# Eight stage buffers instead of four for the projected pieces, and a denser start of their schedule in block 0

## The reference, cut to what matters

```python
h = x + concat(retention(...), window_attention(...)) @ w_out     # columns from rms_norm(x) @ w_in, w_in: 1024 x 2816
xt = rms_norm(h)
q  = (xt @ peer_w_q)                       # 8 heads x 2 halves of 128
s  = einsum(q, peer_sub_keys)              # 128 scores per head and half; top 16, then the best 16 of 256 pairs
idx, gates = ...                           # 128 experts of 16,384 for each token
hh = einsum('thkd,td->thk', peer_u[idx], xt)
a  = gelu(hh) * gates
y  = final_rms_norm(h + einsum('thk,thkd->td', a, peer_v[idx]))
```

## Time and profile before

| | us |
|---|---|
| median of 3 runs | 3061.26 |
| the 3 runs | 3061.08, 3061.26, 3069.75 |
| the profiled execution | 3069.51 |
| its span, first to last instruction | 3067.7 |

### The profile page before, as it was taken

How to read it: one execution, slowest core, us unless ns; L and a number is a source line. 1 busy time by engine, 2 the same in 40 slices (tenths; PEclk the granted TensorE clock), 3 DMA queues, 4 the chain that set the end, 5 groups by cost and what they waited for, 6 DMA issues and landing times.

```text
span 3067.7 us, 29063 instructions
## 1 busy us (share of the span) xinstructions
PE 2262.4 (74%) x8810; PEld 972.3 (32%) x8810; DVE 2035.3 (66%) x4942; ACT 1024.9 (33%) x3215; POOL 1188.2 (39%) x1052
## 2 busy tenths in 40 slices
PE   8888969877798777866687567756785568678564
PEld 6566713554235532332222122212221122211111
DVE  2483446865578655788558965697568765886865
ACT  2222522334233243323433343233432342332322
POOL 0022234424443333433344444444444444444442
PEclk9999988988799888966788788978887789879867
DMA  8589999999999999989999999999999999999997
GB/s 325 195 323 380 347 418 408 422 384 379 420 418 421 371 390 421 415 367 387 423 421 421 407 421 421 418 403 422 421 418 404 416 421 419 402 409 422 418 408 322
DMA packets 194446, 1213.93 MB, mean 396 GB/s; under 512 B 25384, under 2 KB 44368, under 8 KB 60144
## 3 DMA queue, kind: packets, MB, share of 16 engines
q0 software_dynamic: 148608, 1082.20, 86.0%
q1 hardware_dynamic: 45680, 129.87, 11.0%
HBM read 1192.28 MB, written 20.23 MB: 395 GB/s over the span
## 4 chain that ended last, share of the span: by engine, by line
DMA 38%; PE 34%; DVE 14%; issue 6%; ACT 4%; POOL 3%; SPq 1%; POOLq 0%; DVEq 0%; ACTq 0%
DMA ring<-in_peer_uv,idxg 31%; PE ps L916 15%; PE ps L878 7%; DVE ring L1651 7%; PE ps L659 6%; DMA proj_scratch<-wo 5%; POOL ring L584 3%; PE ps L859 2%; ACT ring L980 2%; DVE columns L1505 1%; DVE columns L1556 1%; DMA wo<-in_w_in 1%; PE ps L676 1%; DVE columns L1498 1%; PE ps L632 1%
## 5 line engine op out<-in xcount | busy, mean ns | idle before, releaser
L584 POOL DMA_INDIRECT ring<-in_peer_uv,idxg x1024 | 1172.8, 1145 | 1663.8 <-PE ps L916 1421.2
L916 PE MATMUL ps<-ring 128*64 128x512 f32 x4096 | 1242.2, 738 | 661.9 <-ACT ring L980 660.8
L1651 DVE SCALAR_TENSOR_TENSOR ring<-ring,xlo 128x1024 f32<-128x1024 f32 x512 | 626.6, 1224 | 412.9 <-DMA ring<-in_peer_uv,idxg 402.9
L1651 DVE SCALAR_TENSOR_TENSOR ring<-ring,xhi 128x1024 f32<-128x1024 f32 x512 | 626.3, 1223 | 389.7 <-DMA ring<-in_peer_uv,idxg 380.5
L916 PEld LDWEIGHTS ps<-ring 128*64 128x64 f32 x4096 | 291.1, 158 | 1458.8 <-ACT ring L980 987.2
L1161 ACT ACTIVATE small<-small 128x2 f32<-128x2 f32 x512 | 103.9, 203 | 1577.2 <-DVE ring L1651 1572.9
L659 PE MATMUL ps<-wo 128*128 128x176 f32 x1728 | 304.2, 334 | 72.5 <-ACT wo L980 45.7
L659 PEld LDWEIGHTS ps<-wo 128*128 128x128 f32 x1728 | 280.1, 203 | 135.6 <-issue 71.7
L980 ACT ACTIVATE ring<-gdiag,small 128x64 f32<-128x64 f32 x1024 | 300.3, 340 | 16.8
L980 ACT ACTIVATE gdiag<-fold,gateg 128x64 f32<-128x64 f32 x1024 | 292.8, 333 | 1.5
L878 PE MATMUL ps<-keyw,work 128*128 128x512 f32 (+1 forms) x576 | 268.8, 611 | 1.1 <-ACT work L980 1.1
(11 more groups left out here) (199 smaller groups left out, 1541.2 us busy)
## 6 DMA issues: line engine op xcount, KB each, us to landing
wo<-in_w_in SPq DMA_DIRECT2D x44, 704.0 KB
ring<-in_peer_uv,idxg POOLq DMA_INDIRECT x1024
wo<-in_w_out SPq DMA_DIRECT2D x4, 4096.0 KB
columns<-proj_scratch SPq DMA_DIRECT2D x7, 1536.0 KB, 12.8
ring<-in_w_in SPq DMA_DIRECT2D x7, 1408.0 KB, 8.0
proj_scratch<-wo SPq DMA_DIRECT2D x112, 88.0 KB
ring<-in_wqT SPq DMA_DIRECT2D x16, 512.0 KB, 4.1
h<-in_x_prompt SPq DMA_DIRECT2D x9, 512.0 KB, 8.3
```

The source lines that it names most:

```text
L584: nc.gpsimd.indirect_dma_start(row[r], None, A["peer_uv"], bass.IndirectOffsetOnAxis(ap=experts, axis=0)).then_inc(ld_row[r], 16)
L916: mm = nc.tensor.matmul(acc[side * HP:(side + 1) * HP, n * 512:(n + 1) * 512], row_u[r][:, 0:HP], row_v[r][:, n * 512:(n + 1) * 512], star ...
L1651: ins = stt(row_u[r], row_u[r], 1.0, (xlo, xhi)[unit % 2][:], ALU.mult, ALU.mult, accum_out=dot[:, r:r + 1])
```

## The change

Eight stage buffers take the place of four (five in `wo`, three in a new tensor `stg_more`), and so eight store semaphores the place of four. The ticks of pieces 8 to 47 are new: 16 pieces (q 8 to 23) stand at ticks 1 to 13, where 12 stood, and 24 pieces (q 24 to 47) at ticks 14 to 43, where 28 stood up to tick 44. The ticks of loads and stores follow from these. Pieces 48 to 127 keep their ticks, with eight buffers.

```diff
-STG = 4
+STG = 8
@@ def late_tick(q):
     if q < EARLY:
-        return 1 + (q - AHEAD) * 9 // 8
+        return 1 + (q - AHEAD) * 13 // 16 if q < 24 else 14 + (q - 24) * 31 // 24
@@
+        stg_more = sb("stg_more", [P, 3 * LW])
@@
         xT_early = part(3 * D)
-        stg_early = [part(LW) for _ in range(STG)]
+        stg_wide = [stg_more[:, i * LW:(i + 1) * LW] for i in range(3)]
+        stg_early = [part(LW) for _ in range(STG - 3)] + stg_wide
@@
         xT_late = part(4 * D + KC * SPAD)
-        stg_late = [part(LW) for _ in range(STG)]
+        stg_late = [part(LW) for _ in range(STG - 3)] + stg_wide
```

## The result

The changed kernel takes 3045.84 us (median of 6 runs, 3042.02 to 3050.84), the kernel before 3062.51 us (6 runs beside them). The ratio is 0.9940, 95% interval 0.9924 to 0.9957: 18 us faster, between 13 and 23 (the medians lie 16.7 us apart). Forecast were -23 us and 3038 us; the time lies in the range. Timed once more later, the ratio was 0.9941 (0.9925 to 0.9957).

What follows compares the result with a forecast made beforehand. Nearly the whole kernel was taken as bound by the bytes its gathers bring through saturated DMA engines (421 GB/s). Block 0's -11 and the late pieces' -6 and -6 make -23 us, from 3061.3 to 3038 us, range 3024 to 3060.

Steps and rivals of the forecast that it cites:

- the ceiling of 43 us for 153 us of waits: Whole kernel: ACT's store waits total 152.8 us, but lost DMA rate behind them caps the gain at some 43 us.
- The late pieces, -12 us: Two groups of late pieces at the ends of blocks: store waits go, -6 us each, bounds 0 and 14.4 and 14.6.
- the two dips that it took: Late pieces: rate dips of 9.3 and 9.0 us following the longest store waits; two thirds counted as gain, -6 us each.
- The two at the turns: Late pieces: dips of 5.1 and 5.6 us put down to the block's turn itself and left out of the gain.
- Block 0, -11 us: Block 0's early pieces: the last piece comes at 369 instead of 380 us, -11 us, bounds -20.8 and +2.
- The store waits that go in this part are hidden by the saturated engines, so I count no gain: Block 0's dense front, pieces 8 to 23: removing store waits there was priced at no gain.
- PE's own time for the four, 10 us, lies in PE's idle time there: Block 0's front: four added pieces, 4 x 2.6 = 10 us on PE, fit its idle time (busy 48.9 of 70 us).
- +5 was forecast for the front: Block 0's front: added weight loads and stores and later weights bring pair 7 at 259 instead of 254.02 us.
- Behind pair 7: 126 to 110 us forecast: Block 0, pair 7 to last early piece: PE's work gives 107 us, transfers 110.5; 110 taken instead of 126.
- The saving of 8.4 us: Block 0 behind pair 7: PE's idle times of 4.31 and 4.09 us, both behind ACT's store waits, were to go.
- the slow rival: Block 1's columns land late behind piece 23 and hold DVE's dots; at 297 us, +11, 3072 us; chance 0.06.
- The cover of 3 to 6 us: Block 0: columns landing at about 270 us leave some 3 to 6 us before pair 10 at about 276; priced at 0.

Runs made afterwards that it cites:

- ticks only: The kernel before with the new ticks and still four stage buffers: 3068.92 us, ratio 1.0019 to the kernel before.
- late on four: The changed kernel, but pieces 48 to 127 use four stage buffers again, pieces 0 to 47 keep eight: 3057.27 us, ratio 0.9983 to the kernel before.
- thin weights: Nine weight loads of block 0's front cut from 704 to 88 KB: 3036.47 us against the changed kernel, 3034.28 us with eight buffers and old ticks.
- its twin: The kernel before with eight stage buffers for the late pieces (48 to 127) only, old ticks and four buffers for pieces 0 to 47: 3050.68 us, ratio 0.9952.
- the buffers alone: The changed kernel with the old ticks, so eight stage buffers only: 3045.54 us, ratio 0.9953 to the kernel before.
- columns early: Eight buffers and old ticks, with block 1's columns set to load in block 0 at tick 12 instead of 14: 3044.92 us, ratio 0.9928.

## Why the prediction was right, and which steps were not

- **The bound, and the ceiling of 43 us for 153 us of waits: held.** All 152.8 us went and 18 came back as time. That the rest was hidden behind the ring's eight gathers is the account of the prediction; what the rows show is that ACT now waits 1658.6 us for DVE's dots, where it waited 1572.9, so more than half of the wait turned into one for the dots. DVE's own waits for gathers did not grow (783.4 to 779.4 us).
- **The late pieces, -12 us: right.** Blocks 1 to 3 by profiles with four buffers there (three: before, ticks only, late on four) take 378.5, 374.1 and 348.7 us on the mean, with eight or six (seven, without the thin weights) 372.5, 366.5 and 349.2. The sum is -13.1. By whole runs it is 13 (0.9983 to 0.9940) and 15 (0.9952). The prediction's own sum of lost rate, in the moved windows, gives 9.3 to 3.4 and 9.0 to 3.4 us for the two dips that it took, -6 each as forecast. The two at the turns, which it left, gave 1 and 2 us more (389 to 397 and 374 to 393 GB/s).
- **Block 0, -11 us: the term that was too large.** p24 fell by 10.5 us from the before profile and 7 from its twin; block 0 from 440.0 and 436.9 to 429.5 and 430.1, on the mean -8.7. The sum of lost rate agrees: 20.8 us before, 12.1 in the moved windows (3.7, 2.3 and 6.2 us), again -8.7. By whole runs it is less: buffers and ticks for the early pieces together are worth 5.2 us (0.9983, interval 1.2 to 9.2), and beside late pieces on eight 3.4 (0.9952 to 0.9941, one batch, intervals overlapping). That is where the forecast of -23 and the 18 measured part.
- **"The store waits that go in this part are hidden by the saturated engines, so I count no gain": wrong.** In the front the buffers alone bring pair 7 from 75.1 and 71.5 to 67.1 and (columns early) 65.8, 4 to 9 us. Of the 8.0 us against the kernel before, 3.8 are idle time of PE and 4.2 busy time for the same twelve pieces, at a granted clock of 0.92 instead of 0.89. The mean of 420 GB/s there showed only that transfers were queued, not that the pairs could not have used them earlier.
- **"PE's own time for the four, 10 us, lies in PE's idle time there": wrong.** The tick tables differ by 10 us at pair 7 with full weights, 11 with thin ones. The idle time was there and mostly stayed: 21.1 us before (17.0 in its twin), 17.3 with the buffers only, 15.8 and 15.0 with the new ticks as well. With the buffers only it is 7.3 us ahead of pairs 0 and 1 and 10.1 us of waits for weights, and the four pieces filled 2 of it; the other 10 us came on top. Nor were late weights what the front paid for, as reckoned: PE's waits for them are 10.1 us with the old ticks and 9.1 with the new. The front also lost its saturation, 419 to 400 GB/s, which fits pairs, and with them gathers, that come later. The errors cancelled, and that pair 7 came where it was forecast is luck: +5 was forecast for the front, +2 to +5 measured (77.2 and 76.6 against 75.1 and 71.5), made of -4 to -9 by the buffers and +10 by the ticks. Pair 3 came 9.4 and 6.9 us later, where 12 were reckoned.
- **Behind pair 7: 126 to 110 us forecast, 114 measured** (p24 less p7: 126.7 to 114.1, twice). Counted to the end of the last early piece, as the prediction did, it is 125.0 to 109.3; that flatters, since this piece now stands a pair earlier. Neither half brings the 12.6 us alone: with the buffers only the stretch stays at 127.7, with the ticks only it is 123.0. So beside eight buffers the ticks are worth 13.6 us, beside four 3.7. The saving of 8.4 us that I gave to the store waits there did not come by itself, since the columns' wait took their place, and with the columns landing earlier (125.3) 7.9 us of waits for weights did.
- **So the new ticks move work rather than save it.** With eight buffers they cost 10 us ahead of pair 7 and give back 14 behind it; block 0 is 4 us shorter in the profiles, and the whole (0.9940 and 0.9941 against 0.9953) does not tell them from nothing. The medians are 3045.84, 3045.27 and 3045.54 us.
- **The columns: on the way to the slow rival.** They were to land at 270 and landed at 281.25; counted from the residual 97 us instead of 91. They went out 80 us behind the residual, 2 earlier than the forecast had it, but took 17.2 us, where about 9 were assumed from the 8.6 of before. Pair 10 waited 4.86 us and its matmuls then took 3.68 us instead of 1.94. The prediction had named a landing after 275 as a sign of being wrong, and it came: 281.25, or 275.7 on the start of the kernel before. The cover of 3 to 6 us was gone, as its rival said, but it cost little: without that wait block 0 is 3 us shorter and the whole no faster (0.9944). The rival's threshold, 295, was far.
- **The marks.** ACT's store waits 0 (under 20 forecast); pair 7 at 261.7 (257 to 262) and the last early piece done at 371.0 (364 to 374), both on a start 5.6 us later; on the start of before they are 256.1, just under the range, and 365.4; from the residual of block 0, those of blocks 1 and 2 came 10.5 and 15.5 us earlier (11 and 17); 384, 392 and 389 GB/s (over 355). PE's waits for weights grew only from 7.1 to 9.1 us.

## What to carry to other kernels

A wait on the chain of waits is worth what the transfers lose behind it, not its length; sum the shortfall of GB/s against the saturated rate for the ceiling, then part it by stage. But do not conclude the reverse: an engine's idle time in a saturated stretch is no room for more work when it is spent on waits that stay, here for weights and for the first pair. Four pieces put beside 17.3 us of such idle time moved the next marks by 10 us. When a step is moved ahead in an in-order engine's list, price it by its full duration at the next pair.

## What was not expected of the hardware

The load of 1.5 MB that took 8.6 us in the before profile (256.27 to 264.90) took 17.2 us in the changed kernel, 12.6 with buffers and early columns, and 19.0 with the buffers only (253.64 to 272.68), all beside saturating gathers: the landing of one transfer varied by more than the terms argued over here. (These are times from the issue to DVE's first use.)

A pair's eight matmuls took 1.94 us where the granted clock was 1.00 (261.68 to 263.62 us of the changed kernel), at the level of 2.4 GHz. Behind 4.86 us of idling of PE they took 3.68 us at 0.50, the level of 1.2 GHz, and behind 10.43 us, with the buffers only, again 3.68 at 0.50. In the kernel before, behind 4.31 us, they took 2.71 us at 0.69, between the two levels.
